# Sums of weights for two blocks at a time on two engines, stores from ScalarE's queue, and a down product in sliding runs

## The reference

```python
h = rms_norm(x, prm['ln_mlp'])
return x + jnp.square(jax.nn.relu(h @ prm['w_up'])) @ prm['w_down']
```

## Time and profile before

| | us |
|---|---|
| Median of three runs (2926.2 to 2934.97) | 2933.0 |
| The profiled execution | 2929.14 |
| Its span | 2927.4 |
| First matmul of the MLP starts | 1266.0 |
| Its last one starts | 2903.5 |
| PE busy in the span | 2594.0 (89%) |
| DVE busy | 1715.9 (59%) |
| ACT busy | 1091.9 (37%) |
| POOL busy | 1319.0 (45%) |

### The profile page before, as it was taken

One profiled execution on the slowest core, in us unless ns is written; L12 is line 12 of the kernel. 1 busy time (PEld: TensorE's weight loads), 2 busy tenths in 40 slices (PEclk: granted clock), 3 DMA queues, 4 the chain that ended last, 5 costly groups with the idle time before them and its releaser, 6 DMA issues.

```text
span 2927.4 us, 53308 instructions
## 1 busy us (share of the span) xinstructions
PE 2594.0 (89%) x19701; PEld 2436.6 (83%) x19701; DVE 1715.9 (59%) x2432; ACT 1091.9 (37%) x1633; POOL 1319.0 (45%) x1650
## 2 busy tenths in 40 slices
PE   7889999997997889978898888888778898989897
PEld 6779999996775579977888888888778888888887
DVE  4432225536774785365555555556677767676665
ACT  3242112226663453243333333333433333343444
POOL 0000000000000311167766666766677787888795
PEclk9999999998998889998998999899899999999999
DMA  5154333322017442213333333333444344343432
GB/s 204 58 191 137 93 93 89 83 72 77 30 46 228 137 139 94 91 55 121 124 113 112 119 119 117 124 118 110 161 139 120 119 115 137 112 138 115 138 86 98
DMA packets 324784, 334.59 MB, mean 114 GB/s; under 512 B 28613, under 2 KB 308563, under 8 KB 320438
## 3 DMA queue, kind: packets, MB, share of 16 engines
q1 hardware_dynamic: 321910, 297.56, 33.2%
q0 software_dynamic: 1728, 33.56, 3.1%
q10 hardware_dynamic: 1040, 2.10, 0.2%
HBM read 290.91 MB, written 50.53 MB: 117 GB/s over the span
## 4 chain that ended last, share of the span: by engine, by line
POOL 30%; issue 15%; PE 15%; DVE 5%; POOLq 1%; DMA 1%; ACT 1%; SPq 0%; DVEq 0%; ACTq 0%
POOL q_raw L2716 13%; POOL q_raw L2714 8%; POOL q_raw L2719 8%; PE PS L682 6%; PE PS L2741 6%; DVE q_lo L2729 1%; ACT q_hi L2725 1%; DMA x_raw<-u_rows 1%; POOLq L2715 1%; POOL ssq_f L3043 0%; DMA sel_t<-in_cache_kv_sel,idx_s 0%; POOLq L2718 0%; DVE x_lo L2819 0%; DVE x_acc L2978 0%; DVE x_acc L2967 0%
## 5 line engine op out<-in xcount | busy, mean ns | idle before, releaser
L2741 PE MATMUL PS<-x_hi,q_hi 128*128 128x260 f32 x3584 | 1075.8, 300 | 214.9 <-ACT stage L2876 109.6
L2741 PE MATMUL PS<-x_lo,q_hi 128*128 128x260 f32 x3584 | 1047.8, 292 | 0.0
L2741 PE MATMUL PS<-x_hi,q_lo 128*128 128x260 f32 x3584 | 1041.1, 290 | 0.0
L2741 PEld LDWEIGHTS PS<-x_hi,q_hi 128*128 128x128 f32 x3584 | 711.7, 199 | 262.3 <-ACT stage L2876 107.9
L2729 DVE TENSOR_TENSOR q_lo<-q_raw,q_hi 128x896 fp32r<-128x896 f32 x512 | 628.9, 1233 | 451.0 <-ACT q_hi L2725 446.8
L2725 ACT ACTIVATE q_hi<-q_raw 128x896 fp32r<-128x896 f32 x512 | 485.3, 950 | 709.1 <-PE PS L2741 561.4
L2741 PEld LDWEIGHTS PS<-x_lo,q_hi 128*128 128x128 f32 x3584 | 713.6, 199 | 0.0
L2741 PEld LDWEIGHTS PS<-x_hi,q_lo 128*128 128x128 f32 x3584 | 711.0, 198 | 0.0
L2716 POOL TENSOR_TENSOR q_raw<-q_raw 128x256 f32<-128x256 f32 x512 | 494.8, 966 | 40.1
L2714 POOL TENSOR_TENSOR q_raw<-q_raw 128x128 f32<-128x128 f32 x512 | 304.6, 595 | 317.8 <-DMA q_raw<-in_w_up 206.4
L2719 POOL TENSOR_TENSOR q_raw<-q_raw 128x128 f32<-128x128 f32 x512 | 424.1, 828 | 40.1
(11 more groups left out here) (486 smaller groups left out, 3152.6 us busy)
## 6 DMA issues: line engine op xcount, KB each, us to landing
q_raw<-in_w_up SPq DMA_DIRECT2D x512, 128.0 KB, 2.1
q_raw<-in_w_down SPq DMA_DIRECT2D x512, 128.0 KB, 2.4
w_raw<-in_w_in SPq DMA_DIRECT2D x160, 256.0 KB, 2.9
u_rows<-stage SPq DMA_DIRECT2D x32, 910.0 KB, 4.1
x_raw<-u_rows SPq DMA_DIRECT2D x32, 910.0 KB, 5.5
w_raw<-in_w_out SPq DMA_DIRECT2D x64, 256.0 KB, 2.9
out_kv_win_s<-in_state_kv_win SPq DMA_DIRECT2D x8, 1022.0 KB, 7.5
win_t<-in_state_kv_win SPq DMA_DIRECT2D x8, 896.0 KB
```

The source lines that it names most:

```text
L2741: mm = e.matmul(PS[:, bank, 0:HN], w, v, start=first and c == 0, stop=last and c == 2)
```

## The change

- Sums: `two_sums` makes the sums of two quads in three operations of twice the elements, over two buffers at once. Of four pairs (d = 0 to 3), GpSimd makes those of d = 1 and 3 (`sums_pool`), VectorE those of 0 and 2 (`sums_dve`). `q_raw` keeps its four buffers; they lie so that one access pattern spans two (`q_far`, `q_near`).
- The store of `stage` and the loads of u rows are issued from ScalarE's queue, the store right behind `up_square`, where it waits for `up_sums`.
- `up_first` and `up_read` stand one quad earlier in the orders of ScalarE and VectorE, and `down_read` too; `up_relu` stands one or two operations later.
- The down product no longer goes by chunks. Block s works on m = (s+1) mod 8 and takes all rows up to s that this m has not had: 39 blocks, mostly of eight quads, with short ones at the start (2, 2, 3, 4, 5, 6, 7) and the end. TensorE's instructions for it are written out, where they were in loops.

```diff
-CHUNKS = ((0, 4), (4, 4), (8, 6), (14, 6), (20, 6), (26, 6))
+FIRST_ENDS = (2, 2, 3, 4, 5, 6, 7, 8)
+LATE_ENDS = {28: 28, 29: 28, 30: 28}
...
+        def q_two(half, first, count, step=1):
+
+            part = list(q_far[:].ap[0]) if half == 0 else list(q_near[:].ap[0])
+            t, apart = (q_far, (A4 - A0 - 2 * OPS) // 4) if half == 0 else (q_near, 1024)
+            pat = [part, [apart, 2], [step * P, count], [1, P]]
+            return bass.AP(t[:].tensor, first * P, pat)
...
+        def two_sums(e, half, uses, done, base):
+
+
+
+            for s in (2 * half, 2 * half + 1):
+                e.wait_ge(*q_land[s](32 * uses))
+            e.tensor_tensor(q_two(half, 6, 1), q_two(half, 7, 1), q_two(half, 0, 1), ALU.subtract).then_inc(done, 1)
+            e.wait_ge(done, base + 1)
+            e.tensor_tensor(q_two(half, 4, 2), q_two(half, 6, 2), q_two(half, 2, 2, step=0), ALU.add).then_inc(done, 1)
+            e.wait_ge(done, base + 2)
+            e.tensor_tensor(q_two(half, 3, 1), q_two(half, 1, 1), q_two(half, 4, 1), ALU.subtract).then_inc(done, 1)
+
+        SUMS_POOL = (1, 3)
+        SUMS_DVE = (0, 2)
...
+        for s_ in range(N_U + N_X - 1):
+            m_ = (s_ + 1) % N_X
+            end_ = FIRST_ENDS[s_] if s_ < N_X else LATE_ENDS.get(s_, min(s_ + 1, N_U))
+            BLOCKS.append((m_, ended_[m_], end_ - ended_[m_], n_))
+            n_ += end_ - ended_[m_]
+            ended_[m_] = end_
...
-                    if z == 5:
-                        u_store(e, p - 2)
...
             def up(p, body=None):
                 for z in range(N_X):
-                    n = p * N_X + (z + 3)
-                    quad_hi(e, n, (z + 3) % N_Q)
-                    if z == 0:
+                    if z == 3:
+                        u_store(e, p - 1)
+                    elif z == 7:
+                        up_first(e, p)
+                    quad_hi(e, p * N_X + (z + 3), (z + 3) % N_Q, p + (z + 3) // 8, (z + 3) % 8)
+                    if z == 2:
                         up_square(e, p - 1)
...
             def up(p, body=None):
                 for z in range(N_X):
-                    n = p * N_X + (z + 3)
-                    quad_lo(e, n, (z + 3) % N_Q)
-                    if z == 1:
+                    if z == 0:
+                        sums_dve(e, p, 2)
+                    elif z == 7:
+                        up_read(e, p)
+                    quad_lo(e, p * N_X + (z + 3), (z + 3) % N_Q)
+                    if z == 0:
+                        up_relu(e, p - 1)
+                    elif z == 2:
                         up_sums(e, p - 1)
+                    elif z == 4:
+                        sums_dve(e, p + 1, 0)
```

More of the change, by code:

```diff
@@ L2769, in mlp_pe @@
                     mul_quad(e, p * N_X + j, j % N_Q, j, j == 0, j == N_X - 1, up_free(p) if j == 0 else ())
[L2770 to L2783, removed]
@@ L2786, in build_program @@
[L2786 to L2800, removed]
@@ L2802, in build_program @@
-        U_AT = (248, 249, 251, 252, 257, 262, 267, 272, 289, 294, 299, 304, 316, 317, 325, 330,
-                362, 363, 364, 365, 373, 378, 410, 411, 412, 413, 421, 426, 458, 459, 460, 461)
-        assert len(U_AT) == N_U and all(U_AT[q] >= u_free_after(q) for q in range(N_U))
+            for b, (m, q0, size, n0) in enumerate(BLOCKS):
+                for j in range(size):
+                    n, q = n0 + j, q0 + j
+                    if n == NEED[q]:
+                        e.wait_ge(*u_lo_rdy(q + 1))
+                    mul_quad(e, n, n % N_Q, q % 8, j == 0, j == size - 1, down_free(b) if j == 0 else ())
@@ new lines, in build_program @@
+        BLOCKS, ended_, n_ = [], [0] * N_X, Q_UP
+        for s_ in range(N_U + N_X - 1):
[4 more added lines that the diff above has]
+            ended_[m_] = end_
+        assert n_ == Q_ALL and ended_ == [N_U] * N_X and [x[0] for x in BLOCKS[-N_X:]] == list(range(N_X))
+        QUADS = [(q0_ + j, m_) for m_, q0_, size_, _ in BLOCKS for j in range(size_)]
@@ new lines, in build_program @@
+        NEED = [Q_UP + next(x for x, (a, _) in enumerate(QUADS) if a == q) for q in range(N_U)]
+        FREE = [Q_UP - N_X + q if q < 8 else Q_UP + max(x for x, (a, _) in enumerate(QUADS) if a == q - 8)
+                for q in range(N_U)]
+        LD_AT = [max(FREE[q] + 1, NEED[q] - 10) for q in range(N_U)]
+        for q in range(1, N_U):
+            LD_AT[q] = max(LD_AT[q], LD_AT[q - 1] + 1)
+        HI_LAG, LO_LAG = 4, 5
+        assert all(LD_AT[q] + LO_LAG < NEED[q] for q in range(N_U))
@@ L2806, in u_load @@
+        ENDS = {n0_ + size_ - 1: b_ for b_, (_, _, size_, n0_) in enumerate(BLOCKS)}
+        FINAL_AT = {n0_ + size_ + 1: m_ for m_, _, size_, n0_ in BLOCKS[-N_X:]}
         def u_load(e, q):
-            e.wait_ge(*q_used(u_free_after(q) + 1))
+            e.wait_ge(*q_used(FREE[q] + 1))
             e.wait_ge(u_kept, 16 * (q + 1))
@@ L2839, in mlp_sp @@
                 up(0, z, first=z < N_Q)
-            for z in range(N_X):
-                up(1, z)
-            with e.Fori(2, N_U) as p:
+            with e.Fori(1, N_U) as p:
                 for z in range(N_X):
                     up(p, z)
-                    if z == 5:
-                        u_store(e, p - 2)
             for x, (q, m) in enumerate(QUADS):
@@ L2850, in mlp_sp @@
                 load_quad(e, n % N_Q, w_d, q * PN, m * PN)
[L2851 to L2854, removed]
         def mlp_pool(e):
[L2857 to L2866, removed]
+            sums_pool(e, 0, 3)
+            with e.Fori(1, Q_ALL // 8 - 6) as p:
+                for d in SUMS_POOL:
+                    sums_pool(e, p, d)
+            for i in range(Q_ALL - 48 - 2, Q_ALL + 8):
+                d = i // 2 + 2
+                if i % 2 == 0 and 2 * d < Q_ALL and d % 4 in SUMS_POOL:
+                    sums_pool(e, d // 4, d % 4)
+                if i - 1 in FINAL_AT and FINAL_AT[i - 1] < N_X - 1:
+                    final_pool(e, FINAL_AT[i - 1])
         def up_first(e, p):
@@ L2923, in mlp_act @@
             for n in range(5, N_X + 3):
+                if n == N_X + 2:
+                    up_first(e, 0)
                 quad_hi(e, n, n % N_Q)
@@ L2945, in mlp_act @@
             up(N_U - 1, u_ops)
-            for n in range(Q_UP + 3, Q_ALL):
-                quad_hi(e, n, n % N_Q)
-                if n == Q_UP + 3:
+            for i in range(Q_UP, Q_ALL):
+                if i == Q_UP + 3:
+                    u_store(e, N_U - 1)
+                if i + 3 < Q_ALL:
+                    quad_hi(e, i + 3, (i + 3) % N_Q)
+                if i == Q_UP + 2:
                     up_square(e, N_U - 1)
-                u_ops(n)
-                if n in ENDED:
-                    final_act(e, ENDED[n] - 1)
+                u_ops(i)
+                if i in FINAL_AT:
+                    final_act(e, FINAL_AT[i])
             final_act(e, N_X - 1)
         def down_read(e, b, first, last):
-            q0, size, m, n0 = BLOCKS[b]
+            m, q0, size, n0 = BLOCKS[b]
             r, d = 5 * N_U + 7 * b, 5 * N_U + 5 * b
@@ L2985, in mlp_dve @@
             for n in range(5, N_X + 3):
+                if n == N_X + 2:
+                    up_read(e, 0)
                 quad_lo(e, n, n % N_Q)
-            up_read(e, 0)
+                if n == 7:
+                    sums_dve(e, 1, 0)
             e.wait_ge(o_rms, 2)
@@ L3010, in mlp_dve @@
             up(N_U - 1, u_ops)
[L3011 to L3020, removed]
+            for i in range(Q_UP, Q_ALL):
+                b, d = ENDS.get(i), i // 2 + 2
+                if i == Q_UP:
+                    sums_dve(e, d // 4, d % 4)
+                elif b is not None:
+                    if b == 0:
+                        e.wait_ge(*u_relu(2 * N_U))
+                    elif b == 4:
+                        e.wait_ge(u_kept, 16 * N_U)
+                    down_read(e, b, b < N_X, b >= N_U - 1)
+                if i + 3 < Q_ALL:
+                    quad_lo(e, i + 3, (i + 3) % N_Q)
+                if i == Q_UP:
+                    up_relu(e, N_U - 1)
+                elif i == Q_UP + 2:
+                    up_sums(e, N_U - 1)
+                if i > Q_UP and i % 2 == 0 and d % 4 in SUMS_DVE and 2 * d < Q_ALL:
+                    sums_dve(e, d // 4, d % 4)
+                u_ops(i)
         y_0rdy, y_T, y_ev_a, y_ev_d, y_rs, y_col, y_ld = (
```

65 lines of the change are left out of this document (33 added, 32 removed).

## The result

The changed kernel takes 2780.3 us in the median, the kernel before 2931.7 beside it: a ratio of 0.948 (0.946 to 0.950), 151 us less. One of its four timed executions took 4803.9 us, for which nothing here gives a cause; the ratio leaves it out, and without it the median is 2778.3. The forecast was 2770. The profiled execution has a span of 2776.5.

What follows compares the result with a forecast made beforehand. No engine is full, so the order of work and its waits bound the MLP stage. First block 42, up product 682 and down product 752 make 1476 us for 1637.5, 161 less: kernel 2770, range 2645 to 2835.

Steps and rivals of the forecast that it cites:

- The hole: Up product: the bank 0 copy waits for the late store; issuing it earlier saves 6 us a block.
- The prices of a pair: Sums of two quads in three operations: 1.6 us on VectorE, 2.94 us on GpSimd.
- the slower rival: GpSimd pays two separated runs as two instructions, 5.9 us a pair; kernel 3128 us; chance 0.06.
- Exclusion: GpSimd and VectorE operations exclude each other; whichever meets the other waits, then takes its own time less 0.14 us.
- the 0.14: Time in us by which an operation that waited for the other engine ends sooner than its own length.
- whole instructions: Rival: the GpSimd/VectorE lock holds full instructions, without the 0.14; 1.05 us more a period, kernel 2836; chance 0.12.
- Exclusion is cheap: Rival: VectorE and GpSimd seldom meet or overlap more; stage 1346 us, kernel 2642; chance 0.25.
- First block: Stage start to first bank 0 copy: 38.1 us becomes 42, as VectorE takes on two or three pairs of sums.
- Up product: First to last bank 0 copy: 31 blocks at a period of 22.0 us, 682 for 806.
- Down product: Last copy to last matmul: 32 periods of 22.5 us, 720, plus 32 for more ends and additions: 752 for 793.
- the two nearest rivals: Cheap exclusion, kernel 2642 us, chance 0.25; lock of whole instructions, kernel 2836 us, chance 0.12.
- The block ends: Down product: 39 blocks for 48, each end saved worth seven reads of PSUM on VectorE, 3.43 us.

Runs made afterwards that it cites:

- e1: The kernel before with only the store of the up product's rows moved to ScalarE's queue, half a block earlier: 2825.4 us, ratio 0.965.
- e5: The changed kernel with the store back in SyncE's queue at its old late place: 2933.7 us, ratio 1.001 to the kernel before.
- e2: The changed kernel with the sums of before, one quad at a time, all on GpSimd: 2760.8 us, ratio 0.943 to the kernel before.
- e3: The changed kernel with GpSimd's sums replaced by memsets that read no memory, so outputs are wrong: 2656.3 us, ratio 0.908.
- e6: The changed kernel with nine eight-quad blocks of the down product cut in two, 48 blocks as before: 2813.6 us, ratio 0.960.
- e9: The changed kernel with the store moved from ScalarE's queue to SyncE's, right behind the load of quad 9: 2759.7 us, ratio 0.942.
- e8: The changed kernel with single-quad sums on GpSimd and the store in SyncE's queue behind the load of quad 9: 2756.0 us, ratio 0.941.
- e7: The changed kernel with VectorE's sums of quads 8 and 9 moved ahead of the q_lo of quad 6: 2743.8 us, ratio 0.937.
- e4: The changed kernel with all pairs' sums on VectorE, none on GpSimd: 2828.0 us, ratio 0.966 to the kernel before.

## Why the prediction was right, and where it was off

**The hole.** Right: the wait is gone, and e1 alone brings 105 of the 151 us. But of the 6 us a block only 3.3 came back in e1; other waits took the rest. That e5 gives back 153 doesn't mean that the other parts are worth nothing: the late store costs more with the new order of the up product (47 us over the kernel before), and the down product keeps its 45. By e1 and e2 the 151 are 105 for the store and 65 for the reads and blocks, less 19 for the new sums.

**The prices of a pair.** VectorE's and GpSimd's were right: 0.73, 1.27 and 0.72 us on GpSimd at the shortest, against 0.74, 1.30 and 0.74. Two separated runs cost nothing extra, so the slower rival had no ground.

**Exclusion.** Right in kind and size. GpSimd's second sum ended 1.16 us behind `up_sums`' first (1654.06 to 1655.22), as the 0.14 has it; whole instructions would give 1.30. The period came out at 22.3 for 22.0; the difference is in the gaps between engines: `q_hi` of quad 6 started 9.84 us into the block, not 9.6, and `q_lo` of quad 2 waited 0.24 for its `q_hi`. "Exclusion is cheap" was the counterfactual of e3: 2642 forecast there, 2656 measured. Two of my signs were poor. I had named a `q_lo` near 1.12 us in the median as the sign of cheap exclusion, and it is 1.09 here, though exclusion is not cheap: most `q_lo`s aren't stretched, and only the mean (1.28 us over `q_far`, 1.10 over `q_near`) shows those that are. And VectorE is at 84 and 81%, not over 85. GpSimd's sum of 512 takes 1.64 us in the mean, 1.27 at its shortest.

**The sum.** Three terms were off and partly cancel. First block: 34.3 us, not 42: VectorE's added sums cost nothing there, as e2, which has none of them, takes 35.8. Up product: 701.5, not 682. Of the 20 us more, 10 are the 0.3 a period, the rest the first (26.2) and the last block (28.2), which a single period can't speak for. In the first, VectorE has a reciprocal of 3.39 us more, but e2's first, with the same reciprocal, is 22.7, so the cause of its length stays open. In the last the first loads of u rows come in, and I had said that they "only cost their instructions". One is issued at 1983.65; the `q_lo` that frees the buffer ends at 1984.55, and GpSimd's sums start 7.17 us later, where the load took 2.89 in the period above:

```profile
1983.65 0.36 ACTq L2838 DMA_DIRECT2D x_raw<-u_rows  x1
...
1991.72 0.74 POOL L2731 TENSOR_TENSOR q_near<-q_near 128x256 f32<-128x256 f32 x1 [11.88 <-DMA q_near<-in_w_up]
```

So a load of weights lands some 4 us later while rows are on their way; that the rows are the cause is read from the times alone. Down product: 749.0 against 752, which is partly luck. Its 19 long blocks in the middle end 21.9 us apart, not 22.5, 11 us less in all, and the short blocks at both ends take back some 8. All three terms end at 1484.8 for 1476. The stated range, 2645 to 2835, shuts out by a few us the times of the two nearest rivals (2642 and 2836), though their chances are counted in its 0.87.

**The block ends.** 3.43 us each forecast, 3.7 measured in e6, so the nine fewer are worth 33 of the 44 us that the down product lost. Of the rest the new sums bring 5 (e2), and some 4 are left for the reads ahead of the `q_lo` and the new order: from e1 to e2, which differ in them and in the nine ends, the down product loses 37. The reads weren't tried by themselves.

**What the prediction didn't see.** It put a price on the new sums but not on leaving them out. e2 has them left out and is 19 us faster. The runs show that this cost comes from the order: with the store out of ScalarE's queue (e9 beside e8) the up product takes 678.2 us with the new sums and 671.0 with the old, 7 apart in place of 26, and e7, which has the new sums in another place, is faster than e2. Why the order of the change costs so much I only read so: on the path, a pair on GpSimd lasts 2.9 us and more under exclusion, and both its quads wait for the end; a single quad's sums last 1.8, and the first of two quads is served earlier. VectorE's 1.6 us and the wait of `q_hi` behind them stand in series with the rest. GpSimd's idle time, 65% of the stage, was no gain in itself. My expectations for e1 and e4 failed on the same side: the timetable was made for one order, and I carried its slack over to others.

**Open.** Why the down product loses 38 us with all sums on VectorE I only argued; and how much of the landing of loads (2.8 to 3.05 us behind a `q_lo`) could be had back wasn't tried.

## What to carry to other kernels

When no engine is full, write the timetable of one period from rows, with loads, queue positions and exclusion in it, and look for the place where an in-order queue holds a transfer back: one store moved half a block ahead brought 105 of the 151 us alone, and with it late the rest brought nothing net. Move work to where its engine already waits (e7, 36 us for one line), and don't take a share of busy time for a bound: halving GpSimd's work cost 19 us in the order in which it came. When several edits come in one change, run the change without each, and then with that part in another place: this one was faster without its most elaborate part (e2), and faster still with the part kept and moved (e7).

## What the runs showed of the hardware

- A GpSimd and a VectorE operation with two SBUF inputs exclude each other, but the one that waited ended about 0.14 us sooner behind the other than its own length: 1.16 us for a sum of 1.30, 0.28 for one of 0.42. GpSimd's memsets left VectorE's sums at 0.42, 0.70 and 0.43 us (e3).
- A transfer's issue holds ScalarE's queue for 0.34 us, and its wait holds all that stands behind it: with the store in SyncE's queue (e9) copies are 21.5 us apart in place of 22.3.
- GpSimd's operations over two runs far apart in a partition cost what one run of the same length costs: 0.73 us for 2x128 elements, 1.27 for 2x256, against 0.74 for 256 and 1.29 for 520 in one run.
